# A thirteenth block pair in each layer, gate rows ahead of the weights, and own buffers for two V weights

## The reference

```python
for l in range(DEPTH):                                   # 2
    mod = (c_act @ w_ada[l] + b_ada[l])[:, None, :]      # 1024 -> 6 x 1024
    sh1, sc1, g1, sh2, sc2, g2 = jnp.split(mod, N_MOD, axis=-1)
    h = rms_norm(x, norm1_g[l]) * (1.0 + sc1) + sh1
    proj = h @ w_in[l]                                   # 1024 -> 7 x 512
    ...
    mix = jnp.concatenate([y_conv, y_ret], axis=-1) @ w_out[l]
    x = x + g1 * mix
    h2 = rms_norm(x, norm2_g[l]) * (1.0 + sc2) + sh2
    x = x + g2 * (jnp.square(jax.nn.relu(h2 @ w_up[l])) @ w_down[l])
return rms_norm(x, final_g)
```

## Time and profile before

| | |
|---|---|
| median of 3 runs | 1175.89 us (1174.18 to 1177.21) |
| profiled execution | 1174.89 us, span 1173.1 us |
| granted TensorE clock, mean | 0.989 |
| TensorE busy | 1137.6 us, 97% |
| VectorE busy | 845.3 us, 72% |
| ScalarE busy | 558.2 us, 48% |
| GpSimd busy | 182.1 us, 16% |
| DMA | 163.01 MB, mean 139 GB/s |

### The profile page before, as it was taken

The page is one execution under the profiler, slowest core; times in us unless marked ns, Lnnn a source line. Parts: engine busy times, 40 slices in busy tenths (PEclk is TensorE's granted clock), DMA queues, the critical chain, the costliest instruction groups (busy, mean ns, idle before and its releaser), DMA issues.

```text
span 1173.1 us, 19843 instructions
## 1 busy us (share of the span) xinstructions
PE 1137.6 (97%) x6554; PEld 1000.3 (85%) x6554; DVE 845.3 (72%) x1255; ACT 558.2 (48%) x923; POOL 182.1 (16%) x140
## 2 busy tenths in 40 slices
PE   4999999999999999999999999999999999999996
PEld 2788888998798989989987888889978989989896
DVE  6877887577878687686578777776779576675754
ACT  6554444246445454454445545434544464554631
POOL 4385010320000000000215801104000000000003
PEclk7999999999999999999999999999999999999998
DMA  9773334342643343432255433424253233232312
GB/s 354 296 287 144 125 107 144 108 145 90 211 147 121 133 161 125 143 116 98 91 180 221 155 128 125 145 100 133 91 198 121 78 101 114 89 115 82 98 63 73
DMA packets 47076, 163.01 MB, mean 139 GB/s; under 512 B 5536, under 2 KB 7712, under 8 KB 46752
## 3 DMA queue, kind: packets, MB, share of 16 engines
q1 hardware_dynamic: 47008, 162.18, 39.9%
HBM read 160.06 MB, written 2.10 MB: 138 GB/s over the span
## 4 chain that ended last, share of the span: by engine, by line
PE 84%; DVE 5%; issue 4%; DMA 3%; ACT 3%; SPq 1%; POOL 0%; DVEq 0%; ACTq 0%; POOLq 0%
PE ps L347 19%; PE ps L349 19%; PE ps L348 19%; PE ps L500 7%; PE ps L502 7%; PE ps L501 7%; DMA w_raw<-weights 3%; PE ps L593 1%; PE ps L578 1%; PE ps L387 1%; DVE ada_raw L965 1%; PE ps L389 1%; PE ps L388 1%; DVE x L1099 1%; ACT w_hi L672 1%
## 5 line engine op out<-in xcount | busy, mean ns | idle before, releaser
L954 DVE TENSOR_TENSOR w_lo<-w_raw,w_hi 128x1024 fp32r<-128x1024 f32 (+1 forms) x194 | 232.4, 1200 | 203.0 <-ACT w_hi L672 201.9
L672 ACT CAST w_hi<-w_raw 128x1024 fp32r<-128x1024 f32 x196 | 196.0, 1002 | 107.2 <-PE ps L349 70.1
L347 PE MATMUL ps<-h_hi,w_hi 128*128 128x512 f32 (+1 forms) x576 | 213.7, 371 | 3.1 <-DVE w_lo L954 2.4
L347 PE MATMUL ps<-u_hi,w_hi 128*128 128x512 f32 (+1 forms) x576 | 211.7, 368 | 1.6 <-DVE x L1099 1.6
L348 PE MATMUL ps<-u_lo,w_hi 128*128 128x512 f32 (+1 forms) x576 | 210.8, 366 | 0.0
L349 PE MATMUL ps<-h_hi,w_lo 128*128 128x512 f32 (+1 forms) x576 | 210.7, 366 | 0.0
L348 PE MATMUL ps<-h_lo,w_hi 128*128 128x512 f32 (+1 forms) x576 | 210.6, 366 | 0.0
L349 PE MATMUL ps<-u_hi,w_lo 128*128 128x512 f32 (+1 forms) x576 | 210.5, 365 | 0.0
L1518 POOL TENSOR_TENSOR ssum<-ssum,buf_a 128x256 f32<-128x256 f32 (+1 forms) x56 | 50.4, 901 | 782.2 <-ACT buf_a L700 781.3
L1099 DVE SCALAR_TENSOR_TENSOR x<-ps,mod,x 128x512 f32<-128x512 f32 (+1 forms) x168 | 105.5, 668 | 43.7 <-PE ps L349 43.7
L347 PEld LDWEIGHTS ps<-h_hi,w_hi 128*128 128x128 f32 x576 | 108.6, 189 | 21.5 <-DVE w_lo L954 2.8
(11 more groups left out here) (172 smaller groups left out, 2173.3 us busy)
## 6 DMA issues: line engine op xcount, KB each, us to landing
w_raw<-weights SPq DMA_DIRECT2D x200, 512.0 KB, 3.4
ada_raw<-ada SPq DMA_DIRECT2D x80, 512.0 KB, 4.9
arena<-ada SPq DMA_DIRECT2D x16, 512.0 KB, 15.2
x<-xT SPq DMA_DIRECT2D x2, 1024.0 KB, 6.6
tab<-tables SPq DMA_DIRECT2D x2, 1024.0 KB, 14.1
outT<-x SPq DMA_DIRECT2D x8, 256.0 KB, 2.3
tab<-tables SPq DMA_DIRECT2D x1, 512.0 KB, 14.7
ident<-identity SPq DMA_DIRECT2D x1, 64.0 KB, 1.9
```

The costliest lines, as they stand in the source:

```text
L347: nc.tensor.matmul(out, wh, hi, start=first, stop=False, skip_group_check=True)
L672: nc.scalar.copy(w_hi[:, j, cols], w_raw[:, j, cols]).then_inc(w_hi_done, 1)
L954: nc.vector.tensor_tensor(w_lo[:, j, cols], w_raw[:, j, cols], w_hi[:, j, cols].bitcast(F32), ALU.subtract).then_inc(w_lo_done, 1)
```

## The change

- **A thirteenth pair.** `PAIRS` is 13. The second plain step's two up units are gone; their two tiles are made by a pair with p = 0, directly behind the first down projection. The T and S sums that it needs, and the rounding of them, move one step ahead on ScalarE and VectorE. The body of the loop over pairs becomes a function `pair_step`, called once ahead of the loop and four times in it.
- **Gate rows.** Rows 24 to 27 are loaded ahead of the weights of step 8, rows 28 to 31 among and behind these, and no longer among the weights of steps 9 and 10. Rows 24 to 29 are reduced in the output projection: one behind each of the four splits, two behind the first two half residuals. Rows 30 and 31 are reduced in the first pair's body. In layer 1 there are no later rows; in layer 0 the rows from 32 on move along with the pairs.
- **V weights.** Two of the four V weights of layer 1 are split into buffers of their own, `v_hi` and `v_lo` (in the place of T sums that are no longer needed), ahead of the last down projection's residuals, and no longer within `between`. The first two Q/K weights can then be loaded and split before V is done. For the second pair of token tiles the V product over four weights at once becomes two over two weights.

```diff
-PAIRS = 12
+PAIRS = 13
@@ sync
                 for j in range(SLOTS):
                     load_weight(l, 7, j)
                     load_ada(b0 + (20 + j), j, 2 if j < 2 else SLOTS)
-                load_step(l, 8, 0, 0)
-                for i in range(2):
-                    load_step(l, 9 + i, 4, b0 + (24 + 4 * i))
+                for j in range(SLOTS):
+                    load_ada(b0 + (24 + j), j, SLOTS)
+                for j in range(SLOTS):
+                    load_weight(l, 8, j)
+                    if j < 2:
+                        load_ada(b0 + (28 + j), j, SLOTS)
+                for j in range(2):
+                    load_ada(b0 + (30 + j), j, 2)
+                load_step(l, 9, 0, 0)
+                load_step(l, 10, 0, 0)
@@ tensor
                 for k in range(4):
                     pe.wait_ge(xs_lo, xs + (KT + k + 1))
                     for t in (2, 3):
-                        v_tile(k, t, (0, SLOTS), k == 0, False)
+                        v_tile(k, t, (0, 2), k == 0, False, own=True)
+                        v_tile(k, t, (2, SLOTS), False, False, own=True)
...
-                for i in range(2):
-                    for j in range(2):
-                        pe.wait_ge(evac_act, ea + (EA_UP + 2 * i + j + 1))
-                        unit(u0 + (U_PLAIN + 4 * i + j), j, 2 * i + j, h_hi, h_lo)
-                    down(u0 + (U_PLAIN + 4 * i), xs + (XS_U + CHUNK), ed + (2 + ED_DOWN + 4 * i), 0)
+                for j in range(2):
+                    pe.wait_ge(evac_act, ea + (EA_UP + j + 1))
+                    unit(u0 + (U_PLAIN + j), j, j, h_hi, h_lo)
+                down(u0 + U_PLAIN, xs + (XS_U + CHUNK), ed + (2 + ED_DOWN), 0)
+                pair(u0 + (U_PLAIN + 4), l, 0, ea + EA_PAIR)
+                down(u0 + (U_PLAIN + 4), xs + (XS_U + CHUNK), ed + (2 + ED_DOWN + 4), 0)
@@ scalar, in between
-                split_hi(l, step, 0)
-                split_hi(l, step, 1)
+                if which:
+                    split_hi(l, step, 0)
+                    split_hi(l, step, 1)
@@ scalar, behind first_step
+                for j in range(2):
+                    relu(4 + j, j, U_PLAIN + j)
+                    split_hi(l, 10, j, slice(T, D) if j else slice(0, D))
+                    u_square(4 + j, 0, EA_UP + 4 + j + 1)
+                    t_high((T3, T1)[j])
+                    u_high(4 + j, 0, 4 + j)
+                    t_high((T2, T4)[j])
+                for index, at in enumerate((S3, S1, S2, S4)):
+                    s_high(0, at, index + 1)
+                split_hi(l, 10, 2)
@@ scalar, ahead of down_square
+                        nc.scalar.copy(v_hi[:, j, :], w_raw[:, j, :]).then_inc(w_hi_done, 1)
@@ vector, in between
-                split_lo(l, step, 0)
+                if which:
+                    split_lo(l, step, 0)
                 tiles(0, 0, 1)
-                if which == 0:
-                    split_lo(l, step, 1)
@@ vector, output projection
                 for j in range(SLOTS):
                     pe_has(l, U_OUT + j)
                     residual(j, j, M_GATE1)
                     split_lo(l, 7, j)
+                    ada_pair(l, 12 + j // 2, M_GATE2 + j // 2 * 2, j % 2, later=True)
...
                 for j in range(SLOTS):
                     dve.wait_ge(pe_half, l * 16 + j + 1)
                     residual(SLOTS + j, OUT_BANK[0][j], M_GATE1, HALVES[0])
+                    if j < 2:
+                        ada_pair(l, 14, M_GATE2 + 4, j, later=True)
@@ vector, behind t_second
-                gate_pair(12, M_GATE2)
-                split_lo(l, 10, 0)
                 u_low(4, 0, 4)
-                t_low(T3, 1)
-                split_lo(l, 10, 1)
-                u_low(5, 0, 5)
-                t_low(T2, 2)
-                gate_pair(13, M_GATE2 + 2)
...
-                gate_pair(14, M_GATE2 + 4)
-                gate_pair(15, M_GATE2 + 6)
...
+                raw_loaded(10)
                 s3_sum()
                 s1_sum()
                 s2_sum(0)
                 s4_sum(0)
+                split_lo(l, 10, 0)
+                t_low(T3, 1)
+                t_low(T2, 2)
+                split_lo(l, 10, 1, slice(T, D))
+                u_low(5, 0, 5)
                 t_low(T1, 3)
                 t_low(T4, 4)
                 for index, at in enumerate((S3, S1, S2, S4)):
                     s_low(0, at, index + 1)
+                split_lo(l, 10, 2)
@@ vector, pair_step
+                    if q == 0:
+                        gate_pair(15, M_GATE2 + 6)
...
+                pair_step(0, 0)
+                with dve.Fori(0, 3) as i:
+                    for q in range(1, 5):
+                        pair_step(i, q)
@@ vector, behind split_lo(l, 23, 3)
+                with dve.If(l < DEPTH - 1):
+                    for j in range(2):
+                        dve.wait_ge(w_hi_done, l * UNITS + (25 * SLOTS + j + 1))
+                        nc.vector.tensor_tensor(v_lo[:, j, :], w_raw[:, j, :], v_hi[:, j, :].bitcast(F32), ALU.subtract
+                                                ).then_inc(w_lo_done, 1)
```

More of the change, by code:

```diff
@@ L55 @@
 U_PLAIN, U_PAIR, U_LAST = 40, 48, 96
[L57 removed]
+EA_QK, EA_HEAD, EA_UP, EA_PAIR = 0, 8, 16, 22
 EA = EA_PAIR + 3 * PAIRS
@@ L379, in spread, with v_tile @@
                 nc.tensor.matmul(ps[:, RMS, at], ones[:], ssum[:, at], start=True, stop=True).then_inc(rinv_ps, 1)
-            def v_tile(k, t, units, start, last):
+            def v_tile(k, t, units, start, last, own=False):
                 a, b = units
@@ L385, in v_tile @@
                 hh, hl = h_hi[:, k, t * P:(t + 1) * P], h_lo[:, k, t * P:(t + 1) * P]
-                wh, wl = w_hi[:, a:b, k * P:(k + 1) * P], w_lo[:, a:b, k * P:(k + 1) * P]
+                high, low = (v_hi, v_lo) if own and b == 2 else (w_hi, w_lo)
+                wh, wl = high[:, a:b, k * P:(k + 1) * P], low[:, a:b, k * P:(k + 1) * P]
                 nc.tensor.matmul(out, hh, wh, start=start, stop=False, skip_group_check=True)
@@ L398, in v_end @@
                         for t in tiles:
-                            mm = v_tile(k, t, units, False, k == KT - 1)
+                            mm = v_tile(k, t, units, False, k == KT - 1, own=xs is not None)
                             if k == KT - 1 and t < 3 and units[0]:
@@ L414, in v_step @@
                             for t in part:
-                                mm = v_tile(k, t, units, units[0] == 0 and k == 0, k == KT - 1)
+                                mm = v_tile(k, t, units, units[0] == 0 and k == 0, k == KT - 1, own=True)
                         if units[0]:
@@ L927, in _ @@
+                pair_step(0, 0)
+                with act.Fori(0, 3) as i:
+                    for q in range(1, 5):
+                        pair_step(i, q)
+                split_hi(l, 23, 3)
+                with act.If(l < DEPTH - 1):
+                    for j in range(2):
+                        act.wait_ge(w_in[j], (l * STEPS + 24) * 16 + 32)
+                        pe_has(l, U_LAST - 3)
+                        nc.scalar.copy(v_hi[:, j, :], w_raw[:, j, :]).then_inc(w_hi_done, 1)
                 added = l * SQ + SQ_MIX
@@ new lines, in _, with pair_step, pair_has, next_rows @@
+                split_lo(l, 10, 2)
+                def pair_step(i, q):
+                    p, step = i * 4 + q, i * 4 + (10 + q)
+                    tile = 2 * q + 6
+                    def pair_has(count):
+                        dve.wait_ge(pair_ps, l * (6 * PAIRS) + i * 24 + (6 * q + count))
+                    if q == 1:
+                        dve.wait_ge(mod_added, l * 24 + 24)
+                    residuals(i * 16 + (U_PAIR - 8 + 4 * q), q % 2)
+                    split_lo(l, step, 3)
+                    def next_rows():
+                        with dve.If(l < DEPTH - 1):
+                            gate_pair(i * 3 + (15 + q), i * 6 + 2 * q - 2)
+                    if q == 0:
+                        gate_pair(15, M_GATE2 + 6)
+                    if q in (1, 2):
+                        next_rows()
+                    if q == 3:
+                        with dve.If(i < 2):
+                            next_rows()
+                    def next_early():
+                        raw_loaded(step + 1)
+                        pair_has(2)
+                        s3_sum()
+                        pair_has(5)
+                        s1_sum()
+                        s2_sum(p + 1)
+                    def next_late():
+                        pe_has(l, i * 16 + (U_PAIR + 4 * q - 3))
+                        s4_sum(p + 1)
+                    def next_low():
+                        for index, at in enumerate((S3, S1, S2)):
+                            s_low(p + 1, at, index + 1)
+                    if q < 4:
+                        next_early()
+                    else:
+                        with dve.If(i < 2):
+                            next_early()
+                    pair_has(6)
```

(30 more changed lines are left out.)

181 lines of the change are left out of this document (59 added, 122 removed).

## The result

The changed kernel takes 1181.67 us (median of 4 runs, 1179.69 to 1183.16) against 1175.91 us (4 runs, 1174.18 to 1177.21) for the kernel before: a ratio of 1.0054, 95% interval 1.0041 to 1.0067. It is slower, by 5.8 us. The profiled execution took 1179.69 us, span 1177.8, so 4.8 us more than that of before; it is the fastest of the four.

A forecast was written before the change was run, and what follows sets the result against it. TensorE, busy 97% of the span, bounds the kernel: its work plus its holes. Terms +11.4 (output projection), -6.97 (pair stretch) and -0.85 (layer boundary) give +3.6 on 1175.89: 1179.5 us, own range 1177 to 1182, 8-in-10 range 1174 to 1183.

The forecast's parts named there:

- The stretch of the pair: MLP, first down projection to end of first block pair: 31.05 us in each layer, 6.97 us less in all.
- the pair's hole: TensorE's 1.7 us wait inside the first pair for low parts of the S sums; forecast to go.
- Rival C: Output projection collision as forecast, but TensorE's wait inside the first pair stays: +3.2, 1182.7 us; chance 0.10.
- the prediction's walk: VectorE's steps before the first pair: first S low part from 292.2, pair from 291.67, margin 0.3 us, cost nothing.
- The six reductions in the output projection: Gate-row reductions take turns with GpSimd's additions there, delaying the mean of squares 5.7 us a layer, 11.4 in all.
- my walk: Output projection, VectorE and GpSimd step by step, GpSimd first after each split: mean of squares at 241.1 instead of 235.36.
- Rival A: Reductions and GpSimd don't hold each other up in the output projection: 0.75 us a layer, -6.3, 1169.6 us; chance 0.15.
- rival B: Output projection: VectorE's next operation goes ahead of waiting GpSimd; mean of squares 3.7 us late, -0.4, 1175.5 us; chance 0.13.
- What follows the mean of squares: From TensorE's first mean of squares to the first pair, all distances stay the old ones; no cost.
- The boundary of the layers: V step between layers: VectorE's chain 1.14 us shorter, V products 0.3 us more; net 0.85 us less.
- the hole at the loop's start: TensorE's 1.5 us hole at 620.56, looking like the jump back; forecast to stay, no gain, bounds 0 and 1.5.
- rival D: As forecast, but TensorE's hole at the start of the layer loop goes as well: 1178.0 us; chance 0.07.

The follow-up runs named there:

- the second chip: The changed kernel itself, unchanged, run and profiled again beside its variants: 1182.82 us, ratio 1.0076 to the kernel before.
- the first two experiments: Changed kernel with the six reductions moved to other places: 1167.8 us; changed kernel with them in place, reading activated c from PSUM: 1170.45 us.
- the filled one: Changed kernel plus 24 unused products of 256 columns on TensorE ahead of the mean of squares, in both layers: 1178.45 us, ratio 1.0031.
- e5_rows_only: Kernel before with only gate rows 24 to 29 loaded and reduced as in the change, twelve pairs, old V step: 1185.05 us, ratio 1.0092.
- e7_two_back: Changed kernel with the two reductions behind half residuals moved behind the norm's scale and first T sums, four behind splits kept: 1173.77 us, ratio 0.9992.

## Why the prediction was right, and where its sizes were off

I said 1179.5 us, own range 1177 to 1182, the whole range 1174 to 1183, and slower as the likeliest of the three. The median was 1181.67, on the second chip 1182.82.

**The stretch of the pair: right.** -6.97 us forecast, -3.30 and -3.66 measured, and the pair's hole went: its first S low part starts at 299.02 on VectorE, the pair at 298.57. Rival C falls. VectorE begins the S low parts 0.45 us after TensorE begins the pair, and the prediction's walk had 0.53. What it left open is whose gain that is: with the rows moved and no pair the stretch is 31.83 us, so 5.4 of the 7.0 us belong to the rows that left it, their reductions and their loads together, and 1.6 to the pairs. The rows brought 5.4 us by leaving this stretch, and their reductions cost 10.8 us where they went.

**The six reductions in the output projection: the mechanism right, the size 0.3 us a layer too large.** Forecast +5.7, measured +5.39 and +5.38. The holes are 0.79, 0.89 and 3.04 us where I had 1.1, 1.2 and 3.4. Where it differs is the second reduction. In my walk each of GpSimd's additions is waiting when a split ends; at 223.46 it was not, by 0.13 us, the reduction kept its 1.21 and only the 128x2 addition was held (1.02 for 0.16). From there on every step comes some 0.3 us sooner than in the walk, up to the mean of squares. Rival A, that they don't hold each other, and rival B, that VectorE goes first, fall with the three reductions of 2.31 us. What A's condition is worth, the first two experiments show: 7.0 us under the kernel before without the collision by another place, 4.3 us without it at the same place, where A said 6.3.

**What follows the mean of squares: wrong.** The prediction said that all later distances are the old ones. In layer 0 of the profile the distance to the spread is 4.67 us instead of 3.32, because the clock falls to 1.2 GHz behind the hole; filled with products the same wait costs no clock. This term, nothing in my sum, is 1.35 us in the profiled execution (1.25 of it the clock). The changed kernel against the filled one, on different chips but each to its kernel before: 1.0054 and 1.0076 against 1.0031, so 2.7 to 5.3 us for the median. The forecast and the median are 2.2 us apart, so this one term is enough for the difference. Here luck has a part. With the hole filled, and so without the fall, the time is 1.0031 times that of the kernel before, 1179.6 us at its 1175.91, which is my sum of 1179.5 almost to the digit, but just at the line of 1179.4 from which on I called it slower. The prediction had named that closeness (0.33 for slower, 0.22 for no difference); what took the kernel clear of the line is the clock, which it didn't foresee.

**The boundary of the layers: right within what it can show.** The V step came 1.14 us sooner by itself (2.46 us late at 603.90, where the mean of squares of that boundary was 3.60 late), as forecast. The net is -0.56 us in this profile where I said -0.85; in the second profile of the changed kernel it is 622.22 - 584.66 = 37.56 us against 38.46 before, -0.90. The difference is the hole at the loop's start, 1.76 us in one and 1.40 in the other. It stays with all the variants (1.29 to 1.76 us in ten profiles), so rival D falls. One reading was incomplete: outside the first 50 us not all of TensorE's holes before are ended by VectorE; one of 1.99 us at 1164.22, at the end of the program, is ended by GpSimd's sum. It is there in every variant and changes nothing in the sum.

**The sum.** By the profile: 0.1 + 10.8 - 7.0 - 0.6 + 1.5 = 4.8, against 3.6 forecast. The misses are -0.6 (walk), +1.5 (clock and spread), +0.3 (boundary) and +0.1 (start). In the chances, those of "no difference" add up to 0.42 (0.22, 0.13 and 0.07) where I wrote 0.38.

## What to carry to other kernels

Work that is moved out of a stage at its limit isn't placed well by the idle share of the stage that takes it: ask which memory operands it has and which other engine is at work on the same memory there. The same six reductions, in the same part of the kernel, cost 5.4 us a layer beside GpSimd's additions, nothing in VectorE's gaps a few operations away, and some 1.1 us with one operand in PSUM. And a wait of TensorE of two or three us should be priced with what the clock may do behind it, or be filled.

Before crediting an arithmetic saving, run the kernel with only its side effect: here the rows alone brought 5.4 of the 7.0 us of the MLP's stretch, and six rows placed in gaps, without the new pair, are 5.2 of the 7 us that the best version gains. That version, all of the change with the reductions in gaps, is 1167.8 us, 0.6% under the kernel before.

## What the hardware showed

- Where a GpSimd addition is waiting when a VectorE operation on two SBUF operands ends, it goes in between, even if VectorE's next operation is ready: a reduction of 1.21 us takes 2.31. If it is issued 0.13 us after the end, VectorE goes first. So the order on the shared access hangs on a few tenths of a us.
- Behind a hole of 3.0 us on TensorE the granted clock fell to 1.2 GHz in four of six cases, not always in the same layer of the same kernel. Three times the fall came 0.7 to 1.8 us after the hole, lasted 3.4 us and cost 1.25 to 1.50 us; once (`e5_rows_only`, layer 1) it came 0.2 us before the hole's end, lasted 6.8 us and cost 2.73 us. With holes of 0.75 to 0.97 us at the same place it wasn't seen. What decides among the six is open, and 3.0 us is no limit: at the end of the program TensorE waits 2.0 to 2.1 us in all ten profiles, and in `e7_two_back`, after full activity at 1.00, the clock was at 0.50 some 0.4 us behind that hole (1.98 us, ended at 1163.41).
- At the start of the layer loop's second turn TensorE idles for 1.3 to 1.8 us in all ten profiles, and in five of them the profile names no other engine for it ("issue"), so it looks like the jump itself; no run here took the jump away.
